# Two output projections begun inside the scans before them, z products in pieces, expert credits given early, in a float32 two-block kernel

## The reference

```python
h = rmsnorm(x, norm_g[l]) * (1.0 + scale[:, None, :]) + shift[:, None, :]
p = h @ w_in[l]
y = jnp.concatenate([y_rwkv, y_sb], axis=-1) @ w_out[l]
x = x + gate[:, None, :] * y
return rmsnorm(x, final_g)
```

```python
qkv, z, ab = jnp.split(x @ w_in, [GDN_CONV_CH, GDN_CONV_CH + GDN_VAL_WIDTH], axis=-1)
qkv = jax.nn.silu(_dwconv(qkv, conv_w))
# g and beta come from ab; o = forward + backward gated delta rule
o = _rms(o) * norm_w * jax.nn.silu(z)
return o.reshape(bsz, seq, GDN_VAL_WIDTH) @ w_out
```

## Time and profile before

| | |
|---|---|
| median of 3 runs | 1942.95 us (1939.46 to 1948.96) |
| profiled execution | 1940.8 us, span 1939.0 us |
| TensorE busy | 1684.9 us, 87% of the span |
| VectorE, ScalarE, GpSimd busy | 908.0, 658.8, 143.7 us |
| DMA | 211.24 MB, mean 109 GB/s |

### The profile page before, as it was taken

One profiled execution on the slowest core, in us unless ns is written; L12 is line 12 of the kernel. 1 busy time (PEld: TensorE's weight loads), 2 busy tenths in 40 slices (PEclk: granted clock), 3 DMA queues, 4 the chain that ended last, 5 costly groups with the idle time before them and its releaser, 6 DMA issues.

```text
span 1939.0 us, 36639 instructions
## 1 busy us (share of the span) xinstructions
PE 1684.9 (87%) x15053; PEld 1072.5 (55%) x15053; DVE 908.0 (47%) x1896; ACT 658.8 (34%) x1315; POOL 143.7 (7%) x306
## 2 busy tenths in 40 slices
PE   0799999999988888999999999999879966777788
PEld 0446565565663457677676768676744543333333
DVE  5215063350621255868686777778610461111163
ACT  1124151331510254555555555655410111111113
POOL 8201000010000000000000000000000011111100
PEclk9999999999967999999999999999989979999989
DMA  8311030110201221111111121211027419999931
GB/s 324 80 45 46 1 89 1 45 46 1 87 1 54 73 68 43 47 45 45 45 45 44 46 67 40 70 46 44 2 87 274 174 41 380 421 421 411 376 137 43
DMA packets 107703, 211.24 MB, mean 109 GB/s; under 512 B 10382, under 2 KB 78315, under 8 KB 95275
## 3 DMA queue, kind: packets, MB, share of 16 engines
q1 hardware_dynamic: 102352, 200.69, 28.6%
q0 software_dynamic: 4896, 8.40, 1.2%
q10 hardware_dynamic: 316, 0.13, 0.0%
HBM read 203.81 MB, written 14.81 MB: 113 GB/s over the span
## 4 chain that ended last, share of the span: by engine, by line
PE 46%; DMA 10%; DVE 8%; ACT 3%; issue 2%; SPq 0%; POOL 0%; POOLq 0%; PEld 0%; DVEq 0%; PEldq 0%; ACTq 0%
PE ps L1355 11%; DMA arena<-in_moe_w_gate_dram 8%; PE ps L2342 6%; PE ps L1366 4%; PE ps L1119 3%; PE ps L1519 3%; PE ps L1494 2%; PE ps L2862 2%; PE ps L2692 2%; DMA arena<-in_moe_w_up_dram 2%; PE ps L1396 1%; PE ps L1406 1%; PE ps L1418 1%; DVE W L2064 1%; PE ps L1377 1%
## 5 line engine op out<-in xcount | busy, mean ns | idle before, releaser
L1355 PE MATMUL ps<-hT,W 128*128 128x512 f32 x512 | 230.2, 594 | 3.3 <-ACTq L94 2.2
L1355 PEld LDWEIGHTS ps<-hT,W 128*128 128x128 f32 x512 | 94.9, 190 | 100.1 <-issue 98.3
L543 PE MATMUL ps<-hT,W 128*128 128x512 f32 x288 | 141.0, 612 | 4.3 <-DVE spare L187 4.3
L1366 PE MATMUL ps<-W,hT 128*128 128x256 f32 x512 | 117.9, 384 | 0.0
L2342 PE MATMUL ps<-W,yT 128*128 128x512 f32 x256 | 112.2, 601 | 0.9 <-ACT yT L1728 0.9
L1366 PEld LDWEIGHTS ps<-W,hT 128*128 128x128 f32 x512 | 95.3, 191 | 12.9
L1914 DVE SCALAR_TENSOR_TENSOR arena<-ps,arena 128x510 f32<-128x510 f32 (+1 forms) x128 | 95.4, 745 | 13.4 <-ACT arena L1634 10.0
L2692 PE MATMUL ps<-arena,yT 128*32 128x256 f32 x1024 | 63.5, 405 | 28.0 <-DMA arena<-in_moe_w_gate_dram 18.5
L1519 PE MATMUL ps<-W 64*64 64x64 f32 x2304 | 81.8, 224 | 6.0 <-ACT W L1738 6.0
L1494 PE MATMUL ps<-W,arena 64*64 64x64 f32 x2048 | 70.6, 224 | 15.9 <-DVE W L2067 8.3
L2342 PEld LDWEIGHTS ps<-W,yT 128*128 128x128 f32 x256 | 49.3, 193 | 62.7 <-issue 62.7
(11 more groups left out here) (504 smaller groups left out, 3018.9 us busy)
## 6 DMA issues: line engine op xcount, KB each, us to landing
W<-in_w_in_dram SPq DMA_DIRECT2D x33, 512.0 KB, 7.0
W<-in_gdn_w_in_dram SPq DMA_DIRECT2D x16, 1024.0 KB, 7.0
arena<-in_moe_w_gate_dram SPq DMA_DIRECT2D x16, 1024.0 KB, 9.8
arena<-in_moe_w_up_dram SPq DMA_DIRECT2D x16, 1024.0 KB, 13.2
arena<-in_moe_w_down_dram SPq DMA_DIRECT2D x16, 1024.0 KB, 16.6
W<-in_moe_w_up_dram SPq DMA_DIRECT2D x16, 1024.0 KB, 12.1
W<-in_moe_w_down_dram SPq DMA_DIRECT2D x16, 1024.0 KB, 5.9
W<-in_moe_w_gate_dram SPq DMA_DIRECT2D x16, 1024.0 KB, 23.1
```

What stands on the lines that cost most here:

```text
L543: mm = pe.matmul(ps[:, 5 + i % 2, :], w[:, k, j, :], hT[:, k, :], start=(k == 0), stop=(k == ND - 1))
L1355: mm = pe.matmul(ps[:, 6 + k0 % 2, :], wg[:, k, j * P:(j + 1) * P], hT[:, k, :], start=(k == 0), stop=(k == ND - 1))
L1366: mm = pe.matmul(ps[:, 4 if t < 2 else 1, 256 * (t % 2):256 * (t % 2) + 256], hT[:, k, t * P:(t + 1) * P], wz[:, k, :], start=(k == 0), st ...
```

## The change

1. `mixed_part(pe, bank, lo, hi)` runs matmuls lo to hi of one half token tile of the first output projection, in the order MIX, whose last two slices are those that the last pair writes. Twelve go into the last pair's scan (one behind three of the four steps of each chunk), three around the two reductions, nine behind them before the wait for the end of the stage. The rest is run token tile by token tile. Tiles are transposed and copied as they are done, and the gate columns of tiles 0 to 2 are run before the last tile is transposed.
2. The load of x goes behind the last attention product, and the gate weights are loaded into another place behind the attention output. The semaphore that counted the gate weights with three other loads now counts those three (48 instead of 64).
3. z of tile 2 is cut 3 + 5, z of tile 3 is cut 2 + 2 + 4, and v is kept in pieces of two copies.
4. `first_part` runs 20 of the 32 matmuls of the first round of the second output projection inside the last head.
5. The three credits of the expert loop stand at the beginning of the fixed tiles, and ScalarE copies h^T before the next tile's tokens.

```diff
+    MIX = (0, 1, 2, 5, 6, 7, 4, 3)
+    def mixed_part(pe, bank, lo, hi):
+        t, h = bank // 2, bank % 2
+        for i in range(lo, hi):
+            k = MIX[i]
+            mm = pe.matmul(ps[:, bank, :], yT[:, k, t * P:(t + 1) * P], wo1(k)[:, 512 * h:512 * h + 512], start=(i == 0), stop=(i == ND - 1))
+        return mm
...
+                sp.wait_ge(*rw_pe.at("sb O", n))
+                sp.dma_start(xtok[:], a["x"][0].rearrange("(t p) d -> p t d", p=P)).then_inc(x_again, 16)
+                sp.wait_ge(*rw_dve.at("sb y", n))
+                sp.dma_start(wab, g_in[:, :, GDN_AB:GDN_AB + 64]).then_inc(wab_in, 16)
...
+                    at = 4 * c + slot
+                    if at == 0:
+                        pe.wait_ge(o1_in, 16 * ND)
+                    for e in range(12 * at // 16, 12 * (at + 1) // 16):
+                        mixed_part(pe, (5, 6)[e // 6], e % 6, e % 6 + 1)
...
+            if last:
+                mixed_part(pe, 0, 0, 1)
             pe.wait_ge(*rw_act.at("Y", n))
             pe.matmul(ps[:, 7, :], pairs[:], ysb, start=True, stop=True).then_inc(*rw_pe.step("mean"))
             if not last:
                 next_products(n, 40, 44)
+            else:
+                mixed_part(pe, 0, 1, 3)
...
+        def finished(t):
+            for h in range(2):
+                mixed_part(pe, 2 * t + h, 6, ND).then_inc(*o1_pe.step(f"y {t} {h}"))
+        def turn_x(t):
+            pe.wait_ge(*o1_dve.at(f"x {t}"))
+            for k in range(ND):
+                mm = pe.transpose(ps[:, 2 * t + k // 4, P * (k % 4):P * (k % 4) + P], xtok[:, t, k * P:(k + 1) * P], ident[:])
+            mm.then_inc(*o1_pe.step(f"x^T {t}"))
+        mixed_part(pe, 0, 3, 6)
+        mixed_part(pe, 1, 0, 6)
         after(pe, STICK)
-        pe.wait_ge(o1_in, 16 * ND)
-        for t in range(NT):
-            for h in range(2):
-                for k in range(ND):
-                    mm = pe.matmul(ps[:, 2 * t + h, :], yT[:, k, t * P:(t + 1) * P], wo1(k)[:, 512 * h:512 * h + 512],
-                                   start=(k == 0), stop=(k == ND - 1))
-                mm.then_inc(*o1_pe.step(f"y {t} {h}"))
-        for t in range(NT):
-            pe.wait_ge(*o1_dve.at(f"x {t}"))
-        for k in range(ND):
-            for t in range(NT):
-                mm = pe.transpose(ps[:, k, t * P:(t + 1) * P], xtok[:, t, k * P:(k + 1) * P], ident[:])
-            mm.then_inc(*o1_pe.step(f"x^T {k}"))
+        finished(0)
+        mixed_part(pe, 2, 0, 6)
+        mixed_part(pe, 3, 0, 6)
+        finished(1)
+        mixed_part(pe, 4, 0, 6)
+        finished(2)
+        turn_x(0)
+        turn_x(1)
+        mixed_part(pe, 7, 0, 6)
+        turn_x(2)
+        finished(3)
+        pe.wait_ge(wab_in, 16)
+        for t in range(NT - 1):
+            gate_columns(pe, t)
+        turn_x(3)
         o1_pe.close()
...
+        def keep_xT(t):
+            act.wait_ge(*o1_pe.at(f"x^T {t}"))
+            act.activation(hT[:, :, t * P:(t + 1) * P], ps[:, 2 * t:2 * t + 2, :].rearrange("p b (k c) -> p (b k) c", k=4), ACT.Copy)\
+               .then_inc(*o1_act.step(f"hT {t}"))
         after(act, STICK)
         for t in range(NT):
+            if t == 2:
+                keep_xT(0)
+            if t == 3:
+                keep_xT(1)
+                keep_xT(2)
...
+    def gate_columns(pe, t):
+        pe.wait_ge(*o1_act.at(f"hT {t}"))
+        for k in range(ND):
+            mm = pe.matmul(ps[:, 0, 64 * t:64 * t + 64], hT[:, k, t * P:(t + 1) * P], wab[:, k, :], start=(k == 0), stop=(k == ND - 1))
+        return mm
...
-        def z_part(s, t):
-            if t == 0:
+        def z_part(s, t, ks=range(ND)):
+            if t == 0 and ks[0] == 0:
                 pe.wait_ge(*(gz_in.at("in", s.ago.i) if s.ago else (gz0_in, 16)))
                 pe.wait_ge(*s.dve.at("norm eps 0", s.i))
                 pe.wait_ge(*s.dve.at("norm eps 1", s.i))
-            for k in range(ND):
+            for k in ks:
                 mm = pe.matmul(ps[:, 4 if t < 2 else 1, 256 * (t % 2):256 * (t % 2) + 256], hT[:, k, t * P:(t + 1) * P],
                                wz[:, k, :], start=(k == 0), stop=(k == ND - 1))
-            if t % 2:
+            if t % 2 and ks[-1] == ND - 1:
                 mm.then_inc(*s.pe.step("z half" if t == 1 else "z"))
...
+                    if st == 0 and lv == 1:
+                        z_part(s, 2, range(3))
+                    if st == 0 and joined:
+                        z_part(s, 3, range(2))
                     if st == 1 and top:
-                        z_part(s, 3)
+                        z_part(s, 3, range(4, ND))
                     if st:
                         g = st - 1
+                        if g == 1 and joined:
+                            z_part(s, 3, range(2, 4))
...
-                    z_part(s, 2)
+                    z_part(s, 2, range(3, ND))
...
+        gates()
         project(s, k_, 0)
         project(s, k_, 1)
-        gates()
...
+        pe.wait_ge(o2_in[0], 16)
+        first_part(pe, 6, 0, 2)
         solved(s, 0)
+        first_part(pe, 6, 2, 3)
         y_columns(s, True)
         state_update(s, 0)
         attended(s, 0)
         state_products(s, 1)
+        first_part(pe, 6, 3, 4)
         solved(s, 1)
+        first_part(pe, 5, 0, 1)
         state_update(s, 1)
         attended(s, 1)
         state_products(s, 2)
+        first_part(pe, 5, 1, 3)
         solved(s, 2)
+        first_part(pe, 5, 3, 4)
         state_update(s, 2)
         attended(s, 2)
         state_products(s, 3)
+        first_part(pe, 7, 0, 1)
         solved(s, 3)
+        first_part(pe, 7, 1, 2)
         attended(s, 3)
+        first_part(pe, 7, 2, 4)
+        first_part(pe, 0, 0, 4)
+        pe.wait_ge(*s.act.at(f"qS {NT - 1}"))
+        first_part(pe, 2, 0, 4)
         y_columns(s, False)
...
-                    if 2 * lv + g in (5, 6, 7, 8):
-                        keep_v_tokens(s, 2 * lv + g - 5)
+                    for k in {(2, 1): (0, 1), (3, 0): (2,), (3, 1): (3, 4), (4, 0): (5,), (4, 1): (6, 7)}.get((lv, g), ()):
+                        keep_v_tokens(s, k // 2, k % 2)
...
+    def first_part(pe, bank, lo, hi):
+        t, h = bank // 2, bank % 2
+        for k in range(lo, hi):
+            pe.matmul(ps[:, bank, :], yT[:, k, t * P:(t + 1) * P], ring[0][:, k, 512 * h:512 * h + 512], start=(k == 0), stop=False)
...
+                    if c == 0 and 2 * t + h in (0, 2, 5, 6, 7):
+                        continue
...
+        ex["dve"].credit(dve)
...
+        ex["pe"].credit(pe)
         S = ex0["pe"]
         pe.wait_ge(fixed_g[0], 16)
         turn(0).then_inc(*S.step("first xg^T"))
@@ -2736,7 +2809,6 @@
         n_it = iterations(pe)
         S = ex["pe"]
-        S.credit(pe)
...
-            act.wait_ge(*of_tile("pe", i).at(f"xg^T {o}", i))
-            turned(o, S, f"xg^T {o}")
             act.wait_ge(*of_tile("pe", i).at(f"h^T {b}", i))
             act.activation(hgT[:, b, :, :].rearrange("p f t -> p (f t)"), ps[:, 4, 0:2 * P], ACT.Copy).then_inc(*S.step(f"h^T {b}"))
+            turned(o, S, f"xg^T {o}")
+        ex["act"].credit(act)
         act.wait_ge(*ex0["pe"].at("first xg^T"))
         turned(0, ex0["act"], "first xg^T")
         for b in range(2):
@@ -2785,7 +2857,6 @@
         ex0["act"].close()
         n_it = iterations(act)
         S = ex["act"]
-        S.credit(act)
```

32 lines of the change are left out of this document (11 added, 21 removed).

## The result

The changed kernel takes 1858.16 us (median of 4 runs, 1855.54 to 1863.51) against 1942.95 for the kernel before beside it (1939.46 to 1948.96; a fourth run of it, of 4325.8 us, is left out); the ratio is 0.956, 95% interval 0.952 to 0.960. The profiled execution took 1859.54 us with a span of 1857.8: 81.2 us less span than before, where the prediction's sum was 96.

What follows compares the result with a forecast made beforehand. Limits follow one another: matmuls in projections and heads, chains of short waits in the two last scans, transfers in the expert stage. 28 + 27 + 19 + 22 = 96 us off 1940.8 gave 1845, range 1828 to 1868.

Steps and rivals of the forecast that it cites:

- Part 1 (28): Last RWKV scan and first output projection: earlier block end 20.5, shorter tail 3.6, fewer gate columns 4.3, together 28 us.
- That the clock would rise: Last scan: filling matmuls bring the clock from 0.50 to 1.0 from the second chunk, chunk period 7.5 us.
- Part 2 (27): Eight delta-rule heads: z in pieces and v in smaller pieces save 27 us, bounds 13 to 32.
- Sum 3.4 us a head: Each of eight heads: 1.2 and 1.4 us from z plus 0.8 from v, 27 us for eight.
- 0.8 for v: Each head: smaller v pieces take copies out of 0.38 us waits at two levels, 0.8 us with what they pass on.
- 1.2 and 1.4 for z: Each head: net gain of z matmuls in the first level's wait (1.2 us) and around level five (1.4 us).
- rival (b): Heads: z pieces push what they stand before, 1.6 us a head, 13 instead of 27, total 1859; chance 0.14.
- Part 3 (19): Last head and second projection: 20 matmuls moved, 17.4 us, less 1.5 overhang, plus 3 for the clock: 19 us.
- Part 4 (22): Expert stage: earlier credits let loads start sooner, 21.5 us, with half a microsecond per fixed tile from scalar reorder: 22 us.
- rival (c): Expert stage: early transfers only fill both buffer sets, then wait for TensorE; half the head start lost, 1856; chance 0.08.
- The term for what is given back, 3.5: Expert stage: 3.5 of the 24.9 us stay idle while SP waits for the fixed down product.
- Rival (d): Heads: inserted matmuls hold the level chains, the array falls to 1.2 GHz, slower than before, 1960; chance 0.01.

Runs made afterwards that it cites:

- scan_bare: Changed kernel without matmuls in the last RWKV scan; its twelve projection matmuls run in the closing block instead: 1872.6 us, ratio 0.962.
- v_whole: Changed kernel with v copied in four large groups again, z still in pieces: 1856.2 us, ratio 0.954.
- spread_v_pieces: Changed kernel with z of tile 3 spread further (two matmuls before the last two in level 5, two in the top level), v in pieces: 1852.0 us, ratio 0.951.
- after: The changed kernel itself, with all parts of the change: 1858.2 us, ratio 0.956 to the kernel before.
- second_whole: Changed kernel with the 20 early matmuls of the second output projection taken out of the last head, run whole behind it: 1880.4 us, ratio 0.965.
- credits_late: Changed kernel with the three credits of the expert loop back behind the fixed tiles: 1880.2 us, ratio 0.965.
- z_whole: Changed kernel with z whole again at its two old places, v still in smaller pieces: 1891.0 us, ratio 0.973.
- heads_old: Changed kernel with z whole at its old places and v copied in four large groups: 1876.0 us, ratio 0.962.
- tiles_together: Changed kernel with the first projection's end not pipelined: all matmuls, then all four tiles' transposes, then gate columns: 1869.1 us (2 runs), ratio 0.960.

## Why the prediction was right, and where it was not

**Result and range.** 1845 was forecast and 1858 measured, inside 1828 to 1868 and at the edge of the forecast's own spread.

**Part 1 (28).** Held. At the first projection it was 22.3 against 24: the two reductions and the chunks as worked out (7.84 for 7.5), the tail a little longer for the 1.32 us wait of the last tile's copy. At the loop's first head it was 32.0 against 31, and that closeness is luck: the three other kernels with the same code had 25.7 to 28.4. That SP's order for the first head's weights costs nothing held too. That the clock would rise was the step with a rule against it in one reading; scan_bare shows it by taking the matmuls away.

**Part 2 (27): the term that was mis-sized.** "Sum 3.4 us a head" measured 1.8 in the undisturbed head and 1.5 to 1.6 on the mean of the loop's, and the part 12 to 18 us. Two steps failed, about equally. The 0.8 for v "with what they pass on" was 0: v_whole and spread_v_pieces differ from their partners by nothing that can be told. And the 1.2 and 1.4 for z were 0.9 and 0.8: the push on the level behind was 0.4 and 0.9 where "some 0.2 later" and "0.4 pushed" stand. This second step failed in kernels that have no gap, so it is rival (b)'s mechanism, pieces that push, and its 1.6 a head and 1859 are what came. The first step has another cause, a wait that no view of before made prominent: its trace had "<-issue" before L1486 with 2.0 us in all, and I took it for noise. In after the v pieces take away two waits of 0.37 us a head and the gap gives them back. A check was to be had without any experiment: an undisturbed head had 88.0 - 84.0 = 4.0 us of idle TensorE, and a sum of 3.4 claims nearly all of it.

**Part 3 (19).** 20.2 by the points, 22 by second_whole, which also loses clock. The overhangs of "tenths" and the clock at 0.99 were right. The 0.85 us a matmul read from the earlier trace rows was low, because that window ends before the last 16 records (1531.25 to 1538.12); the whole projection of before, 1425.19 to 1538.12, gives 0.88 for each of its 128, against the 0.87 used.

**Part 4 (22).** 18.2 by the points, 20 to 22 by credits_late, so the mechanism and rival (c)'s fall are shown. The term for what is given back, 3.5, is 5.0, and its reason was wrong: the DMA engines are not idle for it (0.99 in both), the transfers take longer. The h^T order's microsecond can't be told from nothing.

**Rival (d)** (clock lost inside the heads) showed up in full only in an experiment, z_whole: every head with a dip, and 15 us over heads_old. In after two gaps are followed by a fall of the clock, at 1074 and 1337 us.

**The sum of the parts undone**, 14 (scan) + 11 (tiles) + 18 + 22 + 22 = 87 by the medians, against 85 for the whole (1942.95 - 1858.16), is close by luck: from the ratios the same parts sum to 62. By the points of the traces they are 11.2 + 6.4 + 13 + 21.5 + 20.0 = 72 of 81.2 us. The three moved matmuls behind the scan and the nine in the wait of the earlier trace rows, 10 us at 0.87 each, were not undone by themselves and would about fill the rest.

## What to carry to other kernels

Before booking hidden work against waits, add up the engine's idle time over the same stretch: it is the ceiling of everything that hiding can give there, clock aside, and a sum near it is too high. Where matmuls are small (32x32 and 64x64, 67 and 109 records with their weight loads in the two microseconds shown above), an idle time marked "issue" in the trace is a limit of its own: look whether it sits at a fixed place of the instruction stream, since a faster chain will only wait there longer, and spread long matmuls ahead of the dense stretch instead of putting them behind it. And a wait that is left open costs more than its length when the clock falls behind it: in the trace of tiles_together 2.27 us cost 6.4, in one execution.

## What the runs showed of the hardware

- TensorE's instructions arrive in packets of 16 KB (256 instructions), 4.2 to 5.9 us apart in the dense stretch shown, and run 2.3 to 2.8 us behind their packet where TensorE waited for it; the gap at a block's boundary was up to 2.0 us.
- A TensorE nop that counts a semaphore took 0.11 us, and 128 of them behind one queued projection were not hidden.
- A granted clock of 0.50 went with a TensorE that was busy all the time: 14.00 of 14.00 us in the gate columns of tiles_together, which began behind a wait of 2.27 us. In after the same matmuls, begun at 1.00 behind the last projection matmuls, ran at full speed (48 records in 5.47 us). The 128x512 matmuls put into the scan brought 1.00.
